# Experts' second block: half rows gathered over 128 partitions, two k tiles in each turn

## The chip, the cores and the metric

The kernel runs on one core of a Trainium2 chip. The metric is device time in microseconds (us) of one execution; a profiled execution also has a span, from its first instruction to its last. Engines are named as the profile does: PE (TensorE) with its weight loads PEld, DVE (VectorE), ACT (ScalarE), POOL (GpSimd), SP (the queue that issues most loads).

## What is computed

One transformer block over 1024 tokens of width 1024: a mixer (attention and a short convolution), then a mixture of 32 experts, four of them for each token. The change lies in the experts:

```python
def moe_ffn(h, w_router, b_router, w_gate_up, b_gate_up, w_down, b_down):
    ...
    top_logits, top_idx = lax.top_k(logits, TOP_K)
    top_w = jax.nn.softmax(top_logits, axis=-1)
    ...
    def expert_block(args):
        xe, e = args
        gu = xe @ w_gate_up[e] + b_gate_up[e]
        gate, up = jnp.split(gu, 2, axis=-1)
        gate = jnp.minimum(gate, SWIGLU_LIMIT)
        up = jnp.clip(up, -SWIGLU_LIMIT, SWIGLU_LIMIT)
        act = gate * jax.nn.sigmoid(SWIGLU_ALPHA * gate) * (up + 1)
        return act @ w_down[e] + b_down[e]
    ...
    y_rows = yb.reshape(n_rows, d) * row_w[:, None].astype(yb.dtype)
    return jnp.zeros_like(hf).at[row_tok].add(y_rows).reshape(bsz, s_len, d)
```

## The kernel before

Stages before the experts: `project_block`, `attention_block` and `mixer_block`. The mixer chooses four experts for each token and writes a list in DRAM, `list_d`, with a region of 1024 entries for each expert; an entry is (token, destination row, index of its weight). The token rows stand in `xn_d`.

`expert_block` (L1577) works through the lists in *groups*, 36 for these inputs. A group holds either one block of 128 entries (called a single turn here) or that and a second block, b = 1, of up to 64 entries (a double turn). Every matrix product is made in float32r from high and low parts, so that a weight half (512 contraction rows by 512 columns) costs block 0 twelve matmuls, `(hi, whi), (hi, wlo), (lo, whi)` for four k tiles, and block 1 eight: its high and low columns stand side by side, 64 and 64, in one stationary tile (`xt2`, `at2`). There are NH = 12 such weight halves in a group, n = 0 to 11: eight for gate and up, four for down.

The engines, each in its own loop over experts and groups:

- SP (L1731) loads the weight halves, 1 MB each, into six buffers, as DVE sets them free.
- ACT (L1887) copies a half to its high part `whi`, DVE (L2013) subtracts for the low part `wlo`, three halves ahead of PE. Both also evict PSUM.
- PE (`body`, L2199) does for each n the matmuls (L2188) and a bias product (L2170). In between it transposes: `xt(1)` (L2128) at the start of a double turn turns the gathered rows of block 1, 8 tiles of 128x128; `turn` (L2138) at n = 6 and n = 9 turns the activations, 4 tiles a block; at n = 10 `xt(0)` (L2128) turns the *next* group's 128 rows, 8 tiles.
- POOL (`body`, L1840) prepares the next group while PE works on this one. In a fixed order: `fetch` (L1767) reads the entries of both blocks from `list_d`; `stored` waits until the scatters of the group before have landed; `aim` (L1812) copies the destination rows; `gather` (L1774) waits for the entries and reads the rows from `xn_d` by an indirect DMA (L1778 is a stand-in of one column for an absent block); `weigh` (L1781) gathers the weights; L1853 copies the next destinations; `store` (L1790) waits for DVE's outputs of the group before and scatters them with an add; L1856 and L1860 end the turn.

Each POOL operation is followed by a wait of POOL for its own completion (`Chain.link`, L31). The entries' wait and the copies ahead of it read:

```python
def gather(b, g, real):
    pool.wait_ge(entry_in[b], 16 * (g + 1))
...
stored(g)
aim(own)
with pool.If(g > 0):
    for b in range(2):
        gather(b, g, b < blocks)
```

Of the kernel before, what the change touches and what calls it, by code (L numbers as in the profile page):

```python
# [6 lines left out]
ALU = mybir.AluOpType  # L7
ACT = mybir.ActivationFunctionType
# [51 lines left out]
def shared(nc, ctx, a, out):  # L60
# [27 lines left out]
    s.list_d = dram("list_d", [s.E * s.T, 3], I32)  # L88
# [15 lines left out]
def project_block(nc, s, a):  # L104
# [39 lines left out]
    with ExitStack() as ctx:  # L144
# [31 lines left out]
        nolist = qhi_all[:, 0:3 * s.E * T // P].bitcast(I32).rearrange("p (n c) -> p n c", c=3)  # L176
# [810 lines left out]
def mixer_block(nc, s, a):  # L987
# [7 lines left out]
    with ExitStack() as ctx:  # L995
# [32 lines left out]
        entry = sb("c_entry", [P, NT, K4, 3], I32)  # L1028
# [55 lines left out]
        with nc.Block() as block:  # L1084
# [45 lines left out]
            def _(pool):  # L1130
# [11 lines left out]
                for col in range(2):  # L1142
# [3 lines left out]
                                        channel_multiplier=K4))  # L1146
                pool.sem_inc(consts, 1)
# [429 lines left out]
def expert_block(nc, s, a, out):  # L1577
# [5 lines left out]
    ROWS = (P, HB)  # L1583
    GU, DN = 2 * F // SL, D // SL
# [10 lines left out]
    with ExitStack() as ctx:  # L1595
# [10 lines left out]
        xg = [sb(f"d_xg{b}", [P, D], F32) for b in range(2)]  # L1606
# [4 lines left out]
        act_t = [sb(f"d_act{b}", [P, SL], F32) for b in range(2)]  # L1611
# [6 lines left out]
        entry = [sb(f"d_entry{b}", [ROWS[b], 3], I32) for b in range(2)]  # L1618
# [4 lines left out]
        two = sb("d_two", [1, 1], I32)  # L1623
        spare = sb("d_spare", [P, 1], F32)
        colf, coli = sb("d_colf", [P, E], F32), sb("d_coli", [P, E], I32)
        turned_x = psum[:, 6:8, :].rearrange("p a (k n) -> p (a k) n", n=P)

# [51 lines left out]
        def groups_ahead(eng, body):  # L1679
# [8 lines left out]
            eng.reg_load(end, s.table[0:1, 0, 1:2])  # L1688
            eng.reg_load(two_at, s.table[0:1, 1, 0:1])
            with eng.Fori(0, E) as e:  # L1690
# [6 lines left out]
                eng.reg_mov(end, next_end)  # L1697
# [15 lines left out]
        with nc.Block() as block:  # L1713
# [44 lines left out]
            def _(pool):  # L1758
                own = Chain(pool, pool_own)
                for b in range(2):  # L1760
                    pool.dma_start(entry[b][:, :], s.list_d[b * P:b * P + ROWS[b], :]).then_inc(entry_in[b], 16)
                own.link(nc.gpsimd.memset(xg[1][HB:, :], 0.0))

                def fetch(b, e, gs, g, real):

                    at = slot_row(pool, e, gs, g, b) if real else 0
                    pool.dma_start(entry[b][:, :], s.list_d[bass.ds(at, ROWS[b]) if real else slice(0, ROWS[b]), :]  # L1767
                                   ).then_inc(entry_in[b], 16)

                def gather(b, g, real):  # L1770
                    pool.wait_ge(entry_in[b], 16 * (g + 1))
                    s.settle(pool)
                    if real:
                        pool.indirect_dma_start(out=xg[b][0:ROWS[b], :], out_offset=None, in_=s.xn_d[:, :],  # L1774
                                                in_offset=bass.IndirectOffsetOnAxis(ap=entry[b][:, 0:1], axis=0)
# [58 lines left out]
                for b in range(2):  # L1834
                    gather(b, 0, True)
# [436 lines left out]
```

## Time and profile before

| | us |
|---|---|
| median of 3 runs | 2335.89 |
| lowest, highest | 2327.54, 2337.54 |
| span of the profiled execution | 2333.4 |
| PE busy | 2204.2 (94%) |
| DVE busy | 1749.8 (75%) |
| ACT busy | 1297.3 (56%) |
| POOL busy | 867.0 (37%) |

Of the profiled execution only the span is given, no time of its own beside it; it is 2.5 us below the median. The experts' loop starts at about 711 us of the span and lasts to its end. A matmul's busy time is its whole length, with several under way at once, so intervals between starts tell more than busy sums. A timeline merges neighbouring rows of one kind: "x8" is eight of them, and its length that of all eight. The text in brackets behind a row is the idle time of its engine before it and what ended that.

### The profile page before, as it was taken

How to read it: one execution, taken by the hardware profiler on the slowest of the kernel's cores; microseconds unless marked ns; L12 is line 12 of the kernel's file. 1: busy time of each engine (PE TensorE's matmuls, PEld its weight loads, DVE VectorE, ACT ScalarE, POOL GpSimd, SP SyncE). 2: the span in 40 equal slices, each digit the busy share in tenths (PEclk: the TensorE clock that was granted, in tenths of full speed). 3: DMA queues.
4: the chain of work that ended last, by engine and by line, in shares of the span. 5: the costliest groups of instructions: out<-in, count | busy, mean ns of one | idle time of the engine just before them, and what ended most of it. 6: DMA issues, size and time to landing. Idle time of an engine off the chain costs nothing.

```text
span 2333.4 us, 36927 instructions
## 1 busy us (share of the span) xinstructions
PE 2204.2 (94%) x10506; PEld 1822.6 (78%) x10507; DVE 1749.8 (75%) x2141; ACT 1297.3 (56%) x1739; POOL 867.0 (37%) x791
## 2 busy tenths in 40 slices
PE   5999997888967999999999999999999999999997
PEld 4778885776756788888888888888888888888886
DVE  5683422776766799977689877787999778799797
ACT  4332212674225577755567755566777556576575
POOL 2262004893235243532224322242344422244251
PEclk9999997999988999999999999999999999999998
DMA  7234205873337899977689967697999868799695
GB/s 259 90 114 149 59 8 141 249 204 116 109 100 261 276 367 372 379 284 238 224 299 375 366 221 236 228 331 258 382 378 375 300 218 296 256 346 382 227 372 168
DMA packets 295170, 583.98 MB, mean 250 GB/s; under 512 B 23936, under 2 KB 45456, under 8 KB 293008
## 3 DMA queue, kind: packets, MB, share of 16 engines
q1 hardware_dynamic: 267456, 510.07, 61.3%
q0 software_dynamic: 26608, 69.07, 10.7%
q10 hardware_dynamic: 1056, 4.19, 0.5%
q8 instruction: 28, 0.46, 0.1%
q14 instruction: 22, 0.18, 0.0%
HBM read 544.79 MB, written 44.24 MB: 252 GB/s over the span
## 4 chain that ended last, share of the span: by engine, by line
PE 68%; issue 1%; DMA 0%; DVE 0%; DVEq 0%; ACT 0%; POOL 0%; ACTq 0%; POOLq 0%
PE psum L2188 62%; PE psum L2170 3%; PE psum L2128 2%; PE psum L2138 2%; DMA d_xg<-xn_d,d_entry 0%; DMA d_entry<-list_d 0%; DVE d_wlo L2013 0%; DVEq L1713 0%; POOL d_spare L1801 0%; ACT d_whi L1887 0%; DVE d_bhl L2105 0%; DVE d_raw L2112 0%; DVE d_xtlo L1992 0%; DVE d_xt L1999 0%; ACT d_xthi L1894 0%
## 5 line engine op out<-in xcount | busy, mean ns | idle before, releaser
L2013 DVE TENSOR_TENSOR d_wlo<-d_raw,d_whi 128x1024 fp32r<-128x1024 f32 x578 | 675.4, 1219 | 118.6 <-ACT d_whi L1887 117.2
L1887 ACT ACTIVATE d_whi<-d_raw 128x1024 fp32r<-128x1024 f32 x578 | 578.8, 1054 | 110.1 <-PE psum L2188 96.3
L2188 PE MATMUL psum<-d_whi,d_xthi 128*128 128x512 f32 x1152 | 454.6, 395 | 5.0 <-issue 5.0
L2188 PE MATMUL psum<-d_whi,d_xtlo 128*128 128x512 f32 x1152 | 449.5, 390 | 0.0
L2188 PE MATMUL psum<-d_wlo,d_xthi 128*128 128x512 f32 x1152 | 449.5, 390 | 0.0
L1790 POOL DMA_INDIRECT out_dram<-d_yst,d_dest x49 | 158.7, 3239 | 719.7 <-DVE d_yst L2060 666.2
L2013 DVE TENSOR_TENSOR d_wlo<-slab,d_whi 128x1024 fp32r<-128x1024 f32 x292 | 343.6, 1218 | 14.0 <-ACT d_whi L1887 12.9
L1887 ACT ACTIVATE d_whi<-slab 128x1024 fp32r<-128x1024 f32 x292 | 292.4, 1054 | 6.7 <-PE psum L2188 6.4
L2188 PEld LDWEIGHTS psum<-d_whi,d_xthi 128*128 128x128 f32 x1152 | 217.1, 188 | 50.4 <-issue 6.9
L2188 PEld LDWEIGHTS psum<-d_whi,d_xtlo 128*128 128x128 f32 x1152 | 216.8, 188 | 45.9
L2188 PEld LDWEIGHTS psum<-d_wlo,d_xthi 128*128 128x128 f32 x1152 | 217.1, 188 | 43.4
L2188 PE MATMUL psum<-d_whi,d_athi 128*128 128x512 f32 x576 | 227.7, 395 | 0.0
L2188 PE MATMUL psum<-d_whi,d_atlo 128*128 128x512 f32 x576 | 224.6, 390 | 0.0
L2188 PE MATMUL psum<-d_wlo,d_athi 128*128 128x512 f32 x576 | 224.4, 390 | 0.0
L2188 PE MATMUL psum<-d_whi,d_xt 128*128 128x512 f32 x384 | 149.7, 390 | 0.2 <-DVE d_xt L1999 0.2
L2188 PE MATMUL psum<-d_wlo,d_xt 128*128 128x512 f32 x384 | 149.7, 390 | 0.0
L1929 ACT ACTIVATE d_athi<-psum 128x512 fp32r<-128x512 f32 x72 | 43.1, 599 | 189.3 <-PE psum L2138 189.3
L1781 POOL DMA_INDIRECT d_rowt<-topw_d,d_entry x72 | 126.7, 1760 | 22.6 <-issue 21.6
L2188 PEld LDWEIGHTS psum<-d_whi,d_atlo 128*128 128x128 f32 x576 | 108.1, 188 | 23.1
L2188 PEld LDWEIGHTS psum<-d_wlo,d_athi 128*128 128x128 f32 x576 | 108.3, 188 | 21.5
L2188 PEld LDWEIGHTS psum<-d_whi,d_athi 128*128 128x128 f32 x576 | 108.4, 188 | 20.1
L2170 PE MATMUL psum<-d_bhl,d_pick 128*128 128x512 f32 (+1 forms) x288 | 115.9, 402 | 2.4 <-DVE d_pick L2066 2.4
(347 smaller groups left out, 3976.2 us busy)
## 6 DMA issues: line engine op xcount, KB each, us to landing
slab<-in_w_gate_up_dram SPq DMA_DIRECT2D x144, 1024.0 KB, 7.5
d_raw<-in_w_gate_up_dram SPq DMA_DIRECT2D x144, 1024.0 KB, 8.1
d_raw<-in_w_down_dram SPq DMA_DIRECT2D x144, 1024.0 KB, 7.2
b_wp<-in_w_ada_dram POOLq DMA_DIRECT2D x16, 1024.0 KB, 8.3
slab<-in_w_in_dram SPq DMA_DIRECT2D x12, 1024.0 KB, 5.4
a_xin<-in_x_dram ACTq DMA_DIRECT2D x2, 2048.0 KB, 14.6
slab<-in_w_ada_dram SPq DMA_DIRECT2D x4, 1024.0 KB, 13.9
v_d<-a_vst POOLq DMA_DIRECT2D x16, 256.0 KB, 2.3
```

Source lines behind the costliest of these rows:

```text
L1781: pool.indirect_dma_start(out=rowt[b][:, :], out_offset=None, in_=s.topw_d[:, :], in_offset=bass.IndirectOffsetOnAxis(ap=entry[b][:, 2:3], ...
L1790: pool.indirect_dma_start(out=s.out, out_offset=bass.IndirectOffsetOnAxis(ap=dest[b][:, :], axis=0), in_=yst[b][:, :], in_offset=None, com ...
L1887: nc.scalar.activation(whi[n % NW][:, part, :], raw[n % NRAW][:, part, :], ACT.Copy).then_inc(whi_ok, 1)
L1929: nc.scalar.activation(athi[:, 4 * i:4 * i + 4, :].rearrange("p k n -> p (k n)"), psum[:, 6, :], ACT.Copy).then_inc(athi_ok, sh)
L2013: nc.vector.tensor_tensor(wlo[n % NW][:, part, :], raw[n % NRAW][:, part, :], whi[n % NW][:, part, :].bitcast(F32), ALU.subtract).then_inc ...
L2128: mm = nc.tensor.transpose(turned_x[:, k, :], xg[b][:, k * P:(k + 1) * P], s.ident[:, :])
L2138: mm = nc.tensor.transpose(psum[:, 6 + b, t * P:(t + 1) * P], act_t[b][:, t * P:(t + 1) * P], s.ident[:, :])
L2170: mm = nc.tensor.matmul(to[0:ROWS[b], :], pick[:, 0:ROWS[b]], bhl[:, at:at + SL], start=False, stop=last)
L2188: mm = nc.tensor.matmul(to, m_[:, KH * h + k, :], w_[n % NW][:, k, :], start=(h == 0 and k == 0 and q == 0), stop=(h == 1 and k == KH - 1 ...
```

## The change

An entry gets a fourth column, twice the token's number. The second block's 64 rows of 1024 columns are gathered as 128 half rows of 512: partition r holds the first half of row r, partition 64 + r the second. For that POOL fetches the block's entries twice, into partitions 0 to 63 and 64 to 127, and adds a constant 0 or 1 to the fourth column (`half_rows`), which gives the index into `xn_halves`. The add, with its wait for block 1's entries, stands in every group, behind the fetches and ahead of `stored` and `aim`. A transposed tile of 128 columns then holds two k tiles of 64 rows, so `xt(1)` has four tiles instead of eight and `turn` two instead of four for block 1. DVE writes block 1's activations in two operations, one to each half of the partitions, and the evictions of the turned tiles read and write them in (s k) order. The memsets of the partitions that were unused fall away. The loop bound that ACT and DVE read ahead goes through a `max` with 1.

```diff
-    s.list_d = dram("list_d", [s.E * s.T, 3], I32)
+    s.list_d = dram("list_d", [s.E * s.T, 4], I32)
...
+                own.link(nc.gpsimd.iota(entry[:, :, :, 3], pattern=[[2 * P, NT], [0, K4]], base=0,
+                                        channel_multiplier=2))
...
+    HELD = ((slice(0, P),), (slice(0, HB), slice(HB, P)))
+    PARTS = (16, 32)
...
-        xg = [sb(f"d_xg{b}", [P, D], F32) for b in range(2)]
+        xg = [sb("d_xg0", [P, D], F32), sb("d_xg1", [P, D // 2], F32)]
...
-        act_t = [sb(f"d_act{b}", [P, SL], F32) for b in range(2)]
+        act_t = [sb("d_act0", [P, SL], F32), sb("d_act1", [P, SL // 2], F32)]
...
-        entry = [sb(f"d_entry{b}", [ROWS[b], 3], I32) for b in range(2)]
+        entry = [sb(f"d_entry{b}", [P, 4], I32) for b in range(2)]
...
+        xn_halves = s.xn_d.rearrange("t (h n) -> (t h) n", h=2)
...
-                eng.reg_mov(end, next_end)
+                eng.reg_alu(end, next_end, 1, ALU.max)
...
                 def fetch(b, e, gs, g, real):
 
-                    at = slot_row(pool, e, gs, g, b) if real else 0
-                    pool.dma_start(entry[b][:, :], s.list_d[bass.ds(at, ROWS[b]) if real else slice(0, ROWS[b]), :]
-                                   ).then_inc(entry_in[b], 16)
+                    if not real:
+                        pool.dma_start(entry[b][0:ROWS[b], :], s.list_d[0:ROWS[b], :]).then_inc(entry_in[b], PARTS[b])
+                        return
+                    at = slot_row(pool, e, gs, g, b)
+                    for rows in HELD[b]:
+                        pool.dma_start(entry[b][rows, :], s.list_d[bass.ds(at, ROWS[b]), :]).then_inc(entry_in[b], 16)
...
+                        src, index = (s.xn_d, entry[0][:, 0:1]) if b == 0 else (xn_halves, turned_at[:, :])
+                        pool.indirect_dma_start(out=xg[b][:, :], out_offset=None, in_=src[:, :],
+                                                in_offset=bass.IndirectOffsetOnAxis(ap=index, axis=0)
                                                 ).then_inc(xg_in[b], 16)
...
-                    own.link(nc.gpsimd.memset(act_t[1][HB:, :], 0.0))
-                    pool.sem_inc(consts, 1)
...
+                def half_rows(own, g):
+
+                    pool.wait_ge(entry_in[1], PARTS[1] * (g + 1))
+                    own.link(nc.gpsimd.tensor_tensor(turned_at[:, :], entry[1][:, 3:4], second_half[:, :], ALU.add))
+
...
                     with pool.If(g > 0):
                         for b in range(2):
                             fetch(b, e, gs, g, b < blocks)
+                        half_rows(own, g)
                     stored(g)
                     aim(own)
...
-                    nc.vector.scalar_tensor_tensor(act_t[b][0:ROWS[b], :], sg[b][:, :], CAP, up[b][:, :],
-                                                   ALU.min, ALU.mult).then_inc(act_ok, sh)
+                    if b == 0:
+                        nc.vector.scalar_tensor_tensor(act_t[0][:, :], sg[0][:, :], CAP, up[0][:, :],
+                                                       ALU.min, ALU.mult).then_inc(act_ok, sh)
+                        return
+                    for n, rows in enumerate(HELD[1]):
+                        cols = slice(n * SL // 2, (n + 1) * SL // 2)
+                        made = nc.vector.scalar_tensor_tensor(act_t[1][rows, :], sg[1][:, cols], CAP, up[1][:, cols],
+                                                              ALU.min, ALU.mult)
+                    made.then_inc(act_ok, sh)
...
-                    for k in range(KT):
+                    for k in range(KT // len(HELD[b])):
                         mm = nc.tensor.transpose(turned_x[:, k, :], xg[b][:, k * P:(k + 1) * P], s.ident[:, :])
                         if k % KH == KH - 1:
-                            mm.then_inc(xt_mm[b], 1)
+                            mm.then_inc(xt_mm[b], b + 1)
...
-                    for t in range(4):
+                    for t in range(4 // len(HELD[b])):
```

On POOL, the preparing part of a single turn before (L1767 the entry fetches, L1812 the copies, L1774 and L1778 the gathers):

```order
L1767 DMA d_entry<-list_d 128x3
L1767 DMA d_entry<-list_d 64x3
L1842 UNCONDITIONAL_BRANCH
L1806 ISA
L1812 COPY d_dest<-d_dest_next 128x1
L34 ISA
L1812 COPY d_dest<-d_dest_next 64x1
L34 REGISTER_ALU
L1847 COMPARE_AND_BRANCH
L1771 REGISTER_ALU
L1774 DMA d_xg<-xn_d,d_entry 128x1024
L1778 DMA d_xg<-xn_d 64x1
```

and in the change (`d_turned_at` is the sum that `half_rows` writes):

```order
L1788 DMA d_entry<-list_d 128x4
L1784 DMA d_entry<-list_d 64x4
L1855 REGISTER_ALU
L1856 TENSOR_TENSOR d_turned_at<-d_entry,d_second_half 128x1
L34 ISA
L1867 UNCONDITIONAL_BRANCH
L1827 ISA
L1833 COPY d_dest<-d_dest_next 128x1
L34 ISA
L1833 COPY d_dest<-d_dest_next 64x1
```

An operation that reads block 1's entries now stands between the fetches and the copies, and the gather (L1795) follows the copies as before; in a double turn's part the second fetch is there twice.

On PE, a double turn at n = 6, before, with the last matmuls of n = 5 ahead (L2138 turns `d_act`, the activations of both blocks):

```order
L2188 MATMUL psum<-d_whi,d_xt 128x512
L2188 MATMUL psum<-d_wlo,d_xt 128x512
L2134 REGISTER_ALU
L2138 MATMUL psum<-ident,d_act 128x128 x8
L2186 REGISTER_ALU
L2188 MATMUL psum<-d_whi,d_xthi 128x512
```

and in the change:

```order
L2218 MATMUL psum<-d_whi,d_xt 128x512
L2218 MATMUL psum<-d_wlo,d_xt 128x512
L2166 REGISTER_ALU
L2168 MATMUL psum<-ident,d_act 128x128 x6
L2216 REGISTER_ALU
L2218 MATMUL psum<-d_whi,d_xthi 128x512
```

Two of eight transposes are gone there and at n = 9, and `xt(1)` at the turn's start has four for eight; nothing else moves on PE.

## Rows read from the trace of the kernel before

**Rows 1.** The chain that ended last, its shares by engine.

```profile
PE 68%; issue 1%; DMA 0%; DVE 0%; DVEq 0%; ACT 0%; POOL 0%; ACTq 0%; POOLq 0%
```

**Rows 2.** Stretch: length, busy us of PE PEld DVE ACT POOL, clock, DMA share, GB/s.

```profile
1218.00:1254.00 36.00, 36.00 (x168) 29.79 (x167) 34.12 (x36) 27.02 (x31) 15.27 (x15) 1.00 1.05 385
1390.50:1451.30 60.80, 60.80 (x286) 50.28 (x285) 43.26 (x51) 32.22 (x41) 16.61 (x15) 1.00 0.70 230
```

**Rows 3.** PE timeline, line L2128: start us, us, engine, line, operation, tiles, count.

```profile
1214.14 1.04 PE L2128 MATMUL psum<-ident,d_xg 128*128 128x128 f32 x8
1250.05 1.04 PE L2128 MATMUL psum<-ident,d_xg 128*128 128x128 f32 x8
```

**Rows 4.** GpSimd timeline of one single turn, same columns, idle before and releaser.

```profile
1223.97 5.33 POOL L1790 DMA_INDIRECT out_dram<-d_yst,d_dest  x1 [11.96 <-DVE d_yst L2060]
...
1236.14 1.09 POOL L1767 DMA_DIRECT2D d_entry<-list_d  x2 [4.15 <-issue]
...
1238.10 0.97 POOL L1812 COPY d_dest<-d_dest_next 64x1 int32<-64x1 int32 x1 [0.16 <-POOL d_dest L1812]
1241.76 1.09 POOL L1774 DMA_INDIRECT d_xg<-xn_d,d_entry  x1 [2.69 <-DMA d_entry<-list_d]
```

**Rows 5.** Entry fetches: count, KB, median us to landing; then the gathers, L1774.

```profile
d_entry<-list_d POOLq DMA_DIRECT2D x36, 1.5 KB, 4.9
d_entry<-list_d POOLq DMA_DIRECT2D x36, 0.8 KB, 4.6
...
DMA to landing us min/median/max: 4.3/6.7/10.4
```

**Rows 6.** One late gather on GpSimd, its use on PE, its landing.

```profile
1664.91 2.01 POOL L1774 DMA_INDIRECT d_xg<-xn_d,d_entry  x1 [2.48 <-DMA d_entry<-list_d]
...
1673.01 1.04 PE L2128 MATMUL psum<-ident,d_xg 128*128 128x128 f32 x8
...
DMA to landing us min/median/max: 8.0/8.0/8.0
```

**Rows 7.** Waits of PE in the loop: total us, times, longest.

```profile
PEld psum L2128 <- DMA d_xg<-xn_d,d_entry: 1.2, 5, 0.3
...
PE psum L2170 <- DVE d_pick L2066: 2.4, 1, 2.4
```

**Rows 8.** An early gather with its use on PE, and all `dest` copies.

```profile
2266.10 1.03 POOL L1774 DMA_INDIRECT d_xg<-xn_d,d_entry  x1 [1.10 <-issue]
...
2275.98 1.04 PE L2128 MATMUL psum<-ident,d_xg 128*128 128x128 f32 x8
...
L1812 POOL COPY d_dest<-d_dest_next x74: 178/964/1149, 725.3 to 2301.1; 128x1 int32<-128x1 int32 x37, 64x1 int32<-64x1 int32 x37
```

**Rows 9.** PE timeline: transposes of a single and of a double turn's activations.

```profile
1237.94 0.60 PE L2138 MATMUL psum<-ident,d_act 128*128 128x128 f32 x4
...
1494.78 1.03 PE L2138 MATMUL psum<-ident,d_act 128*128 128x128 f32 x8
```

**Rows 10.** VectorE timeline at the copy of rows 4 and at rows 9.

```profile
1236.67 2.35 DVE L2013 TENSOR_TENSOR d_wlo<-d_raw,d_whi 128x1024 fp32r<-128x1024 f32 x2
...
1492.20 1.28 DVE L2032 SCALAR_TENSOR_TENSOR d_act<-d_sg,d_up 128x512 f32<-128x512 f32 x2
```

**Rows 11.** Stretches after two PE waits (columns of rows 2), and PE after the longer.

```profile
720.00:725.00 5.00, 2.62 (x12) 1.82 (x10) 4.94 (x5) 2.46 (x4) 0.55 (x1) 1.00 0.00 0
785.00:790.00 5.00, 4.99 (x14) 4.00 (x15) 2.12 (x3) 1.18 (x2) 2.81 (x4) 0.61 0.96 182
...
785.01 0.79 PE L2188 MATMUL psum<-d_whi,d_xthi 128*128 128x512 f32 x1 [5.03 <-issue]
785.61 0.63 PE L2188 MATMUL psum<-d_wlo,d_xthi 128*128 128x512 f32 x1
786.03 0.63 PE L2188 MATMUL psum<-d_whi,d_xtlo 128*128 128x512 f32 x1
```

More of the change, by code:

```diff
@@ L175, in project_block @@
         chanmean = sb("a_chanmean", [P, P], F32)
[L176 removed]
+        nolist = qhi_all[:, 0:4 * s.E * T // P].bitcast(I32).rearrange("p (n c) -> p n c", c=4)
         with ExitStack() as early:
@@ L1027, in mixer_block @@
         iota_e = sb("c_iota_e", [P, E], F32)
-        entry = sb("c_entry", [P, NT, K4, 3], I32)
+        entry = sb("c_entry", [P, NT, K4, 4], I32)
         slot = [sb(f"c_slot{i}", [P, K4], I32) for i in range(2)]
@@ L1687, in groups_ahead @@
             eng.reg_mov(start, 0)
-            eng.reg_load(end, s.table[0:1, 0, 1:2])
+            eng.reg_load(next_end, s.table[0:1, 0, 1:2])
+            eng.reg_alu(end, next_end, 1, ALU.max)
             eng.reg_load(two_at, s.table[0:1, 1, 0:1])
@@ L1696, in groups_ahead @@
                 eng.reg_mov(start, end)
-                eng.reg_mov(end, next_end)
+                eng.reg_alu(end, next_end, 1, ALU.max)
                 eng.reg_mov(two_at, next_two)
@@ L1832, in setup @@
                         pool.wait_ge(y_st[b], ST_CRED)
-                for b in range(2):
-                    gather(b, 0, True)
+                def half_rows(own, g):
+                    pool.wait_ge(entry_in[1], PARTS[1] * (g + 1))
+                    own.link(nc.gpsimd.tensor_tensor(turned_at[:, :], entry[1][:, 3:4], second_half[:, :], ALU.add))
+                gather(0, 0, True)
+                half_rows(own, 0)
+                gather(1, 0, True)
                 setup()
                 start = own.n
-                LINKS = 7
+                LINKS = 8
                 def body(e, gs, g, blocks):
-                    own = Chain(pool, pool_own, start + LINKS * g)
+                    own = Chain(pool, pool_own, start - 1 + LINKS * g)
                     with pool.If(g > 0):
@@ L1852, in body @@
                     for b in range(2):
-                        own.link(nc.gpsimd.tensor_copy(dest_next[b][:, :], entry[b][:, 1:2]))
+                        own.link(nc.gpsimd.tensor_copy(dest_next[b][:, :], entry[b][0:ROWS[b], 1:2]))
                         s.settle(pool)
@@ L1872, in _ @@
                 stored(g)
-                aim(Chain(pool, pool_own, start + LINKS * g))
+                aim(Chain(pool, pool_own, start - 1 + LINKS * g))
                 store(g)
@@ L1899, in xt_two @@
                     act.wait_ge(xt_mm[1], 2 * count)
-                    nc.scalar.activation(xt2[:, :, 0:HB], turned_x[:, :, 0:HB], ACT.Copy).then_inc(xthi_ok[1], 2)
+                    nc.scalar.activation(folded(xt2[:, :, 0:HB]), unfolded(psum[:, 6, :]), ACT.Copy).then_inc(xthi_ok[1], 2)
                 def gated(g, i, b, sh):
```

32 lines of the change are left out of this document (17 added, 15 removed).

## The prediction

> **What bounds the kernel now.** I read first the chain that ended last: TensorE is its largest part by far, 68% of the span, and no other engine reaches 1% [rows 1]. The stretch view says the same of the expert loop. A *single* turn (one block of 128 rows) fills its 36 us with PE work, and a *double* turn (128 rows and a second block of 64) fills its 60.8 us [rows 2]. The granted clock is 1.00 in both, the level of 2.4 GHz. So in steady state every TensorE instruction taken out counts, and every wait put in counts. VectorE has 34.12 of 36 us busy in single turns and 43.26 of 60.8 in double ones. The loads fill the DMA engines in single turns (share 1.05) and not in double ones (0.70).
>
> The PE timeline gives the period of a single turn: the eight transposes of the next turn's rows (`xt(0)`) start 35.91 us apart (1214.14, 1250.05) [rows 3]. There are 36 turns, 12 double and 24 single.
>
> Last I followed GpSimd around one single turn, since it fetches the rows that `xt(0)` needs [rows 4]. `xt(0)` at 1214.14; the scatter of the previous outputs starts at 1223.97, 9.83 later; the entry fetch for the next turn at 1236.14, 12.17 later; the gather at 1241.76, 5.62 later. It lands 6.7 us after its start [rows 5], at 1248.5, and `xt(0)` comes at 1250.05. The ring takes 34.3 of 35.9 us, so **a margin of about 1.6 us is all that the single turns have** although GpSimd looks two thirds idle there. It is less elsewhere: the gather at 1664.91 lasted 2.01 us and landed after 8.0, while PE took the rows at 1673.01, 8.10 after that start [rows 6]. The margin is 0.1, and the wait table already lists five short waits of weight loads for this gather, 1.2 us together [rows 7]. In double turns the same ring stands in 60.8 us, which leaves some 26.
>
> I put together all gathers that PE uses within 12 us. There are 22: 7 like the one at 1241.76 (margin 1.6), 6 like the one at 1664.91 (0.1), and 9, after a double turn or between turns of one expert, like that at 2266.10, used 9.88 later (margin 3.2) [rows 8]. The mean margin is 1.8.
>
> **The change, part by part.**
>
> *Transposes.* A double turn now has 4 instead of 8 in `xt(1)` and 6 instead of 8 in each of its two `turn` places. Eight transposes take 1.03 us and four take 0.60 [rows 9], so one costs 0.43 / 4 = 0.107 us. 8 x 0.107 = 0.86 us for a turn, 12 turns 10.3 us. In the first turn PE then waits 2.4 us for the selection matrix, which VectorE makes [rows 7]; `xt(1)` ahead of it gains nothing there (0.4). That leaves **-9.9 us**, all on the path if nothing else gives way.
>
> *Evictions and activations.* ScalarE's and VectorE's evictions have the same sizes in another order: nothing. The second block's activation on VectorE becomes two operations of half the columns. Two full ones take 1.28 us together, from 1492.20 to 1493.48, and PE turns them at 1494.78 [rows 9, 10]: 1.3 us of cover for some 0.1 us more. VectorE idles 17 us in a double turn. Nothing. If that cover went, the cost would be 24 x 0.1 = 2.4 us, which the range can hold.
>
> *The list with four columns, one more iota, the memsets, the `max` on the loop bound:* before the loop they stand beside waits of GpSimd, and they are tens of ns on other engines in the loop. Nothing, at most 1 us. In the first turn the first gather still waits for the same first entry fetch.
>
> *The new link on GpSimd.* This is the price. Before, each turn issued both entry fetches, did the two `dest` copies while they were in flight, and then waited for entry 0 and gathered. Now `half_rows` stands directly behind the fetches, in every turn, single ones too: it waits for entry **1**, adds, and only then come the wait for the stores, both copies and the gather of block 0. Behind the waiting instruction are queued the copies, both gathers, the weights' gathers and the scatter; the last two have over 10 us before the next outputs, the first gather has its margin.
>
> How late does the gather get? Count from the first fetch. The second fetch starts about 0.55 later (half of 1.09 [rows 4]) and lands 4.6 after that [rows 5], with some 0.5 for the semaphore to be seen (before, the gather starts 5.62 after the fetch, 0.7 after its entry's 4.9, and part of that is its own issue): 5.7. The add has no row. Its nearest rows are the `dest` copies on the same 128x1 columns: 0.178 at least, 0.964 median, 1.149 at most [rows 8]; I take 0.75 since an add on three columns' stride can be no cheaper than a free copy and waits like a copy. Then 0.25 of turnaround, two copies at 0.75 with 0.16 between them, and 1.10 from the last copy to the gather, the idle time of a gather that no longer waits for its entry [rows 8]. 5.7 + 0.75 + 0.25 + 0.75 + 0.16 + 0.75 + 1.1 = 9.45, against 5.62: **the gather comes 3.8 us later**. With every small operation at its shortest it is 2.0 later (5.6 + 0.2 + 0.16 + 0.18 + 0.16 + 0.18 + 1.1 = 7.6), with every one at its longest 4.8.
>
> How long such a small operation takes is set by VectorE: the copy at 1238.10 ended at 1239.07, as the pair of splits that began at 1236.67 ended at 1239.02 [rows 4, 10]. The Trainium skill (SBUF — State Buffer, "SBUF: two separate sides") says that a VectorE operation with two SBUF inputs holds the port pair shared with GpSimd for its whole length and blocks a GpSimd operation that reads SBUF. This trace agrees (0.97 us for a copy that takes 0.178 alone), and by that rule every one of the three small operations would be at its long end, which is a rival below.
>
> *What the lateness costs.* The ring goes by PE's own events, so a wait at `xt(0)` shifts all that follows, outputs and next fetch too, and comes again in the next single turn; there is nothing to catch up with. 7 x (3.8 - 1.6) + 6 x (3.8 - 0.1) + 9 x (3.8 - 3.2) = 15.4 + 22.2 + 5.4 = 43.0 us. Six of these turns are followed by a double one, whose entry 1 comes in two fetches, the third 0.55 later: 6 x 0.55 = 3.3. Longer turns spread the loads, and landings shorten from 6.7 towards the quickest, 4.3 [rows 5]; I take 0.3 of these 2.4 us, as turns lengthen by some 6%: 22 x 0.3 = -6.6. **+39.7 us.**
>
> *The clock.* After the one PE wait of 5.0 us in the loop the next 5 us were granted 0.61: the matmuls start 0.42 us apart there (785.61, 786.03 [rows 11]), while in a single turn they are (36.0 - 16 x 0.107) / 152 = 0.226 apart [rows 2]; eight slow ones cost 1.6 us. After the wait of 2.4 us the stretch stayed at 1.00, the 2.4 GHz level [rows 7, 11]. The six waits of 3.7 lie between; half the price: 6 x 0.8 = **+4.8 us**.
>
> **The sum.** -9.9 + 39.7 + 4.8 = +34.6 us, against the profiled execution's span of 2333.4: 2368.0. The median of the runs, 2335.9, is 2.5 above that span, so the forecast is **2370 us**, 1.5% slower. A measurement of this kernel can tell about 0.5% from no change.
>
> **The rivals.**
>
> *The margin swallows it; only the transposes count.* If the gather comes late by less than its margins, or lands faster by as much, no wait appears, and the time is 2335.9 - 9.9 = 2326 us. For it: at the short end the lateness is 2.0, and the six turns without margin had gathers of 2.01 us where others had 1.04, which may fall back. Against it: the median of the copies is near their long end. It decides at a lateness of 1.8 us, the mean margin; a wait of all 22 at 2.0 would be 7 x 0.4 + 6 x 1.9 = 14 us, little more than the 9.9. Chance 0.2; as 9.9 us are 0.42%, three quarters of this is "no change".
>
> *The small operations are all long, and the clock falls.* At 4.8 us: 7 x 3.2 + 6 x 4.7 + 9 x 1.6 + 3.3 = 68 us, 13 waits of over 3 us with 1.6 us of slow clock each, 21, and -9.9: +79, 2415 us. The Trainium skill (TensorE: Matmul & The Clock Gate, "What's actually happening") has the array's clock gated down by how busy PE has been; the 0.61 agrees with it [rows 11], and it makes this case dearer than its waits. Chance 0.15.
>
> *It lands somewhat earlier or overlaps more than I count.* A lateness near 2.5 gives 7 x 0.9 + 6 x 2.4 + 3.3 - 9.9 = +14, 2350 us. Chance 0.15, part of "slower" and "no change" alike.
>
> *The change doesn't do what it says:* transposes of half the tiles would still be issued. The order of instructions shows 4 and 6 for 8, so this has under 0.01.
>
> **How the numbers follow.** Forecast case (2355 to 2400) 0.5, margin 0.2, all long 0.15, in between 0.15. The likeliest gives 2370. The range takes in the margin case's time and most of the way to the long end, 2326 to 2408. Faster than 2324: 0.06 (a quarter of the margin case). Within 0.5%, up to 2347.6: the rest of that case and a third of the in-between one, 0.19. Slower: 0.75.
>
> **What would show it.** PE's rows on `d_xg` should number 344 instead of 392, and those on `d_act` 336 instead of 384; a double turn should be 0.86 us shorter. Each single turn should start GpSimd's gather 9 to 10 us after the fetch, with the add at 5.7. The wait table should have PE `d_xg` behind its DMA some 20 times, 1 to 4 us each, 35 to 50 in all, and single turns 36 to 40 us long. If that wait isn't there, the ring has a margin that I didn't see, and I am wrong by its whole size; if double turns don't shorten, transposes weren't on the path.

## The result, and the profile after

The changed kernel takes **2362.8 us** (median; 2362.0 to 2363.9), the kernel before 2334.7 in the same rounds: 1.0128 times as long, 95% interval 1.0114 to 1.0142, or 28.1 us more. The profiled execution spans 2361.2 us (before 2333.4).

First the chain that ended last, by engine, in the changed kernel:

```profile
PE 51%; issue 7%; DMA 4%; POOL 4%; POOLq 2%; DVE 1%; DVEq 0%; ACT 0%; ACTq 0%
```

Before, PE alone had 68% and GpSimd none [rows 1]. Now a path through GpSimd and its transfers has a tenth. The view of waits, PE and GpSimd over the expert loop, says where (engine, tile and line waited for, releaser, total us, times, longest):

```profile
POOL d_turned_at L1856 <- DMA d_entry<-list_d: 143.2, 35, 5.3
...
PE psum L2160 <- DMA d_xg<-xn_d,d_entry: 32.5, 13, 3.4
...
PE psum L2200 <- DVE d_pick L2098: 1.8, 1, 1.8
```

Before, only five short waits of weight loads stood there [rows 7]; now the transposes `xt(0)` themselves wait 13 times, 32.5 us in all. The half-row add (L1856) is the instruction that stands waiting for the entries, in every turn that fetches any. Three stretches, with the columns of rows 2: a single turn that ends in a wait, one that doesn't, and a double turn.

```profile
1252.90:1292.10 39.20, 36.05 (x168) 29.53 (x166) 35.81 (x37) 26.91 (x30) 16.18 (x16) 1.00 1.02 373
1216.90:1252.90 36.00, 36.00 (x167) 29.78 (x168) 32.48 (x34) 26.91 (x30) 12.91 (x16) 1.00 1.02 366
1396.70:1456.70 60.00, 60.00 (x277) 49.43 (x276) 43.72 (x53) 32.22 (x41) 14.27 (x17) 1.00 0.71 233
```

The second turn is as long as one before [rows 2], the first is 3.2 us longer at the same PE work, and the double turn is 60.0 us, 0.8 shorter. So turns with and without a wait stand side by side. GpSimd's timeline shows both. The turn with the wait (start us, us, engine, line, operation; idle before it and releaser):

```profile
1262.71 5.31 POOL L1811 DMA_INDIRECT out_dram<-d_yst,d_dest  x1 [11.98 <-DVE d_yst L2092]
...
1274.92 0.56 POOL L1788 DMA_DIRECT2D d_entry<-list_d  x1 [4.24 <-issue]
...
1280.81 1.00 POOL L1856 TENSOR_TENSOR d_turned_at<-d_entry,d_second_half 128x1 int32<-128x1 int32 x1 [4.79 <-DMA d_entry<-list_d]
1282.27 0.68 POOL L1833 COPY d_dest<-d_dest_next 128x1 int32<-128x1 int32 x1 [0.46 <-POOL d_turned_at L1856]
1283.11 0.97 POOL L1833 COPY d_dest<-d_dest_next 64x1 int32<-64x1 int32 x1 [0.16 <-POOL d_dest L1833]
1285.19 1.18 POOL L1795 DMA_INDIRECT d_xg<-xn_d,d_entry  x1 [1.11 <-issue]
```

and the turn ahead of it, without one:

```profile
1226.53 2.03 POOL L1811 DMA_INDIRECT out_dram<-d_yst,d_dest  x1 [9.93 <-DVE d_yst L2092]
...
1235.14 0.56 POOL L1788 DMA_DIRECT2D d_entry<-list_d  x1 [4.22 <-issue]
...
1243.34 1.06 POOL L1795 DMA_INDIRECT d_xg<-xn_d,d_entry  x1 [1.11 <-issue]
```

Fetch to gather is 10.27 us in the first and 8.20 in the second; before it was 5.62 [rows 4]. But the second turn's fetch also comes much earlier: `xt(0)` started at 1216.88, so it is 18.3 us behind it, against 22.1 in the first turn (`xt(0)` at 1252.85) and 22.0 before. Most of this (3.3 us) is the scatter ahead: 2.03 us instead of 5.31. PE at the end of the turn with the wait:

```profile
1288.53 0.39 PE L2218 MATMUL psum<-d_whi,d_atlo 128*128 128x512 f32 x1
1292.07 1.09 PE L2160 MATMUL psum<-ident,d_xg 128*128 128x128 f32 x8 [3.15 <-DMA d_xg<-xn_d,d_entry]
```

What the change saves is there too: the totals of PE's transposes are 344 and 336, as forecast, and four stand where eight did.

```profile
L2160 PE MATMUL psum<-ident,d_xg x344: 270/273/476, 707.4 to 2339.3; 128*128 128x128 f32 x172
...
L2168 PE MATMUL psum<-ident,d_act x336: 270/272/304, 746.8 to 2335.6; 128*128 128x128 f32 x168
```

To compare runs below I use, beside the median, the *loop*: from the start of the first `xt(0)` to that of the last that turns gathered rows, read from PE's timeline (one more behind it turns a stand-in). Before the loop, profiles differ by more than the effects sought (its start lies anywhere from 704.8 to 715.9 us), whatever the kernel. The loop was 1564.9 us before (711.06 to 2275.98) and is 1595.2 now (707.43 to 2302.62), +30.3. Its parts: +32.5 waits; +9.2 slower clock behind 5 of the waits; +1.6 in the first turn; -6.6 because the 5.03 us stall of PE at 785.01 [rows 11] and the slow stretch behind it are absent; -8.7 for the transposes in the 11 double turns behind the first (0.79 each). That makes +28.0; the other 2.3 are spread over the turns, most of them 0.05 to 0.15 us longer. What lengthens the first turn I did not find.

### The profile page after: what moved, and what is told of

It is laid out like the page before. It is cut to its first block, busy times and chain, and to the rows that moved or that the text cites. A ratio compares the mean times of both kernels' runs of the same rounds, so it can differ in the third digit from the quotient of the medians.

```text
span 2361.2 us, 36948 instructions
## 1 busy us (share of the span) xinstructions
PE 2203.7 (93%) x10410; PEld 1816.4 (77%) x10411; DVE 1760.1 (75%) x2165; ACT 1298.4 (55%) x1739; POOL 789.8 (33%) x840
## 3 DMA queue, kind: packets, MB, share of 16 engines
q0 software_dynamic: 27056, 69.26, 10.6%
## 4 chain that ended last, share of the span: by engine, by line
PE 51%; issue 7%; DMA 4%; POOL 4%; POOLq 2%; DVE 1%; DVEq 0%; ACT 0%; ACTq 0%
PE psum L2218 46%; DMA d_xg<-xn_d,d_entry 4%; PE psum L2200 2%; PE psum L2160 2%; PE psum L2168 1%; POOL d_dest L1833 1%; POOL d_roww L1886 1%; POOL out_dram L1811 1%; POOL d_spare L1822 0%; DVE d_yst L2092 0%; POOL d_entry L1788 0%; POOL d_turned_at L1856 0%; POOLq L1682 0%; POOLq L1683 0%; POOLq L1681 0%
## 5 line engine op out<-in xcount | busy, mean ns | idle before, releaser
L1811 POOL DMA_INDIRECT out_dram<-d_yst,d_dest x49 | 127.7, 2607 | 723.3 <-DVE d_yst L2092 718.6
L1955 ACT ACTIVATE d_athi<-psum 128x512 fp32r<-128x512 f32 x72 | 43.1, 599 | 189.7 <-PE psum L2168 189.7
L1802 POOL DMA_INDIRECT d_rowt<-topw_d,d_entry x72 | 96.3, 1337 | 22.6 <-issue 21.6
```

Of the source, the lines that this page charges most:

```text
L1802: pool.indirect_dma_start(out=rowt[b][:, :], out_offset=None, in_=s.topw_d[:, :], in_offset=bass.IndirectOffsetOnAxis(ap=entry[b][0:ROWS[b ...
L1811: pool.indirect_dma_start(out=s.out, out_offset=bass.IndirectOffsetOnAxis(ap=dest[b][:, :], axis=0), in_=yst[b][:, :], in_offset=None, com ...
L1955: nc.scalar.activation(athi[:, 4 * i:4 * i + 4, :].rearrange("p k n -> p (k n)"), psum[:, 6, :], ACT.Copy).then_inc(athi_ok, sh)
```

## The experiments

Two theories stood at the start. **L, the link:** block 0's gather waits behind block 1's entries, the add and the copies, and that alone costs. **H, the half rows:** more descriptors, one fetch more, wider lists and split operations cost. The stall that went with the change was a third thing to explain.

**e1_gather_first**: the changed kernel, with block 0's gather issued ahead of the add (which counts on a semaphore of its own). It computes the same.

```
                     with pool.If(g > 0):
                         for b in range(2):
                             fetch(b, e, gs, g, b < blocks)
-                        half_rows(own, g)
                     stored(g)
                     aim(own)
                     with pool.If(g > 0):
-                        for b in range(2):
-                            gather(b, g, b < blocks)
+                        gather(0, g, True)
+                        half_rows(g)
+                        gather(1, g, blocks == 2)
```

> The changed kernel with one thing moved: block 0's gather is issued ahead of POOL's wait for block 1's entries and the add of the half-row indices, which follow it. Theory L (the link is what costs: block 0's gather waits for block 1's two entry fetches, the add and the two copies): block 0's gather starts 5 to 6 us behind its fetch again instead of 10, PE's 13 waits for d_xg (32.5 us) go, and only the saved transposes are left: before less 8 to 10 us, 2322 to 2330 us. Rival H (the half rows cost: 128 descriptors in place of 64, entries fetched twice, four-column lists, activations in two operations): all of that is still there, and the time stays above 2345 us, with waits of PE in the turns that hold a second block or on DVE. Rival C (the clock lost, whatever starts the gather): above 2345 us with TensorE's granted clock below 0.975.

Measured: 2321.7 us, 0.9943 of before (0.9925 to 0.9960); loop 1553.8. PE's waits in the loop:

```profile
PE psum L2161 <- DMA d_xg<-xn_d,d_entry: 2.7, 1, 2.7
PE psum L2201 <- DVE d_pick L2099: 2.3, 1, 2.3
```

41.1 us of the changed kernel's time go with the moved lines, though every half row is still gathered; the median lies 0.3 us under the expected range. L holds, H falls as far as a kernel without the late gather is concerned. The one wait left is in a turn ahead of a double one, where three entry fetches go out and block 0's gather started 8.3 us behind the first. The five other turns of that kind gather 5.7 to 6.0 us behind it and end in no wait; why this one is late was not looked into.

**e2_wait_alone** and **e3_wait_and_add**: the other way round, the kernel before with the link alone, without and with the add (both also have the `max` on the loop bound, which e4 tests too).

```
                         for b in range(2):
                             fetch(b, e, gs, g, b < blocks)
+                        pool.wait_ge(entry_in[1], 16 * (g + 1))
+                        Chain(pool, half_own, g - 1).link(nc.gpsimd.tensor_tensor(
+                            extra[:, :], entry[1][:, 1:2], entry[1][:, 2:3], ALU.add))
```

> The kernel before with one wait added on POOL: behind the two entry fetches it waits for block 1's entries before it copies the destinations and gathers block 0. No half rows, no add, all transposes as before. (The bound of each expert's turns is also written as a maximum with 1, as the changed kernel has it.) Theory L: the gather starts 8.5 to 9.5 us behind the fetch instead of 5.6, about 0.5 to 1 us earlier than in the changed kernel, and PE waits for d_xg some 13 times by 1.5 to 3 us: 18 to 30 us of waits and 5 to 10 of slower clock, 2355 to 2370 us. Rival H: nothing of the half rows is in it, so the time is that of before, 2330 to 2342 us.

> The kernel before with the wait of the run ahead and behind it one POOL add on 64 rows of the entries, its result unused: the whole new link, without the half rows. Theory L: block 0's gather starts 10 us behind the fetch as in the changed kernel, PE waits about 13 times by 2 to 3.4 us, 30 to 34 us in all, and the transposes that the changed kernel saves (8 to 9 us) are still there: 2366 to 2376 us. Rival H: no more than before, 2330 to 2342 us. If the alternation seen in the changed kernel's trace is a property of the loop (a turn that waits lets the next turn's store and fetch start earlier), waits stand in every other turn here too.

Measured: 2365.2 us (1.0140, 1.0125 to 1.0154) and 2361.9 us (1.0135, 1.0116 to 1.0154), loops 1594.5 and 1593.8. e2 is in its range; e3 was expected 4 us higher at the least. PE's waits in e2, then in e3:

```profile
PE psum L2130 <- DMA d_xg<-xn_d,d_entry: 21.9, 11, 3.2
PE psum L2190 <- issue: 5.0, 1, 5.0
```

```profile
PE psum L2134 <- DMA d_xg<-xn_d,d_entry: 25.2, 12, 2.8
PE psum L2194 <- issue: 5.0, 1, 5.0
```

A single wait for a semaphore costs some 30 us, and **the add costs nothing that the time shows**. In the turn near 1250 us the gather starts 9.22 us behind the fetch in both. GpSimd in e2 shows why, together with e3's row:

```profile
1281.30 1.16 POOL L1813 COPY d_dest<-d_dest_next 128x1 int32<-128x1 int32 x1 [4.73 <-DMA d_entry<-list_d]
1282.63 0.97 POOL L1813 COPY d_dest<-d_dest_next 64x1 int32<-64x1 int32 x1 [0.16 <-POOL d_dest L1813]
```

```profile
1281.57 0.66 POOL L1849 TENSOR_TENSOR d_extra<-d_entry 64x1 int32<-64x1 int32 x1 [4.10 <-DMA d_entry<-list_d]
1282.68 0.68 POOL L1815 COPY d_dest<-d_dest_next 128x1 int32<-128x1 int32 x1 [0.45 <-POOL d_extra L1849]
```

The small operations end in a fixed beat here, so the added one fills time that another spent waiting (e7 below shows the beat). That is not so in every turn: in the one near 1645 us the gather comes 8.06 us behind the fetch in e2 and 9.20 in e3, a beat later. e3's waits are 3.3 us more in all, and its slow stretches of PE 3.0 us less. Here too no two single turns running end in a wait.

**e4_rest_alone**: the small parts alone on the kernel before (four-column list and iota, `max` on the bound, block 1's activation in two).

```
-                    nc.vector.scalar_tensor_tensor(act_t[b][0:ROWS[b], :], sg[b][:, :], CAP, up[b][:, :],
-                                                   ALU.min, ALU.mult).then_inc(act_ok, sh)
+                    for n in range(b + 1):
+                        cols = slice(n * SL // (b + 1), (n + 1) * SL // (b + 1))
+                        made = nc.vector.scalar_tensor_tensor(act_t[b][0:ROWS[b], cols], sg[b][:, cols], CAP,
+                                                              up[b][:, cols], ALU.min, ALU.mult)
+                    made.then_inc(act_ok, sh)
```

> The kernel before with the small parts alone: four-column list entries with their iota, the maximum on the bound of the turns, and block 1's activation as two operations of half the columns. No half rows, no wait added. I costed these at nothing: 2330 to 2340 us, and no new wait on PE. Rival H (the small parts cost): DVE's second activation, 48 of them at about 0.3 us, on the path of the 12 turns with a second block, would give up to 14 us: 2345 to 2350 us.

Measured: 2333.7 us, 1.0000 (0.9989 to 1.0012), loop 1564.8. Nothing, as costed.

**e5_transposes_twice** and **e8_after_twice**: e1 and the changed kernel with each transpose of block 1 issued twice; **e11_half_transposes**: e4 with half of block 1's transposes left out.

```
-                    for k in range(KT // len(HELD[b])):
+                    for k in (k for k in range(KT // len(HELD[b])) for again in range(b + 1)):
...
-                    for t in range(4 // len(HELD[b])):
+                    for t in (t for t in range(4 // len(HELD[b])) for again in range(b + 1)):
```

> The kernel of the run e1_gather_first with each transpose of block 1 issued twice into the same place: PE issues 8 of d_xg and 16 of d_act per turn of two blocks again, as before the change, the last of each pair with the same result. What I hold (T: the transposes are on PE's path, 0.78 us in each of 12 turns; S: the 5.0 us stall of PE near 780 us, in all profiles with the old number of transposes and in neither of those with half of them, belongs to how PE's program is laid out): T alone 2331 us, T and S 2337 us with the stall back, S without T 2328 us. If the half rows' transposes had lain beside other work: 2322 us.

> The changed kernel with each transpose of block 1 issued twice, as the run e5_transposes_twice. If the saved transposes count in the changed kernel as they do without its waits: 2372 us (T) or up to 2379 us with the stall of 5.0 us and the slower clock behind it (S). If the waits for block 0's rows take up what PE saves (the gather's time is set by POOL, not by PE), within 3 us of the changed kernel: 2360 to 2366 us, as the run e3_wait_and_add with its full transposes (2361.9 us) lets one suspect.

> The kernel of the run e4_rest_alone (before, with the small parts) with every other transpose of block 1 left out: 4 of 8 of d_xg and 2 of 4 of each d_act, so half of the second block's columns are not turned and its result is not the layer's. What the change saves on PE, without anything that it adds: by the runs e1 and e5, 0.79 us in each of 12 turns (T, 9.5 us) and the stall with the slower clock behind it (S, 6.7 us): 2317 to 2322 us, no 5.0 us stall, 27 packets. T alone: 2324 us. If these savings need something else of the half rows: 2333 us.

Measured: e5 2334.4 us (1.0004, 0.9994 to 1.0015), loop 1572.2, so 12.7 us above e1 (loop +18.3); e8 2373.0 (1.0172, 1.0147 to 1.0197), loop 1606.0, 10.2 above the changed kernel (loop +10.8); e11 2320.6 (0.9939, 0.9922 to 0.9956), loop 1548.5, 13.1 below e4 (loop -16.3). By the medians of three pairs PE's part of the change is worth 10 to 13 us, and the waits do not swallow it (my suspicion in e8's last sentence was wrong). e5 fell between its 2331 and 2337 us, e8 1 us from its T, e11 into its range. Double turns behind the first are 49.1 us from `xt(1)` to the next `xt(0)` with half the transposes and 49.9 with all, in every pair: 0.8 x 12 = 9.5 us. In the loops of the profiled executions the stall comes on top, 7.0 us for e5 against e1, which with 1.6 us of slow clock behind one wait nearly makes the 18.3. Transposes and stall together, 16.5, are more than the medians give; each median's interval is 2.5 to 6 us either way, so they don't exclude it, and only one execution of each kernel was profiled. In e5, PE in the first single turn, then e5's queue of instruction fetches (packets, MB, share):

```profile
784.65 0.79 PE L2221 MATMUL psum<-d_whi,d_xthi 128*128 128x512 f32 x1 [4.86 <-issue]
...
q8 instruction: 28, 0.46, 0.1%
```

and the same queue in e1:

```profile
q8 instruction: 27, 0.44, 0.1%
```

All kernels with the old number of transposes (before, e2, e3, e4, e5, e8) have 28 packets and the stall; the changed one, e1, e6, e7, e9, e10 and e11 have 27 and none.

**e9_sixteen_more** and **e12_sixteen_signals** ask whether it is the transposes or the length of the code.

```
                     if blocks == 2:
                         pe.wait_ge(xt_ok[0], 2 * (g + 1))
                         xt(1, g + 1)
+                        for n in range(16):
+                            pe.sem_inc(unread, 1)
                     else:
```

> The kernel of the run e1_gather_first with 16 register moves, their result unused, put behind the transposes of d_xg in PE's code for a turn of two blocks: as much code as the 8 transposes that the half rows spare there have with their weight loads (16 instructions), and none of their matrix work. Theory S (the 5.0 us stall is PE's first jump past that code into the code for a turn of one block, and with the shorter code one fetch of instructions less is made): the stall is back in the first turn of one block, the instruction queue shows 28 packets and not 27, the loop is 7 us longer: 2328 to 2332 us. If the stall hangs on the transposes themselves: 2321 to 2324 us with no stall and 27 packets; above that up to 0.8 us in each of 12 turns, should the moves stand on the path.

> The run e9_sixteen_more again with instructions that stay in the program: its register moves had no reader and were not among the executed instructions (36843, as without them). Now 16 increments of an unused semaphore stand behind the transposes of d_xg in PE's code for a turn of two blocks, as many instructions as 8 transposes with their weight loads, with no matrix work. Theory S (the length of that code decides whether one fetch of instructions more is made at PE's first jump past it): the 5.0 us stall of the first turn of one block is back, 28 packets on the instruction queue, the loop 7 us longer than in e1_gather_first and e9_sixteen_more, 2328 to 2332 us. If the transposes' matrix work or data bring the stall: 27 packets, no stall, 2321 to 2325 us, and up to 0.8 us more in each of 12 turns if the increments stand on the path.

e9's moves were optimized away: 36843 instructions ran, as in e1, so it is a repeat of e1 and nothing else (2323.5 us, 0.9953, 0.9937 to 0.9969; loop 1554.9; 1.8 us from e1). e12 measured 2349.5 us, 1.0060 (1.0040 to 1.0080), loop 1581.4. Its PE row in the first single turn, its queue, and its waits of PE:

```profile
781.10 0.79 PE L2220 MATMUL psum<-d_whi,d_xthi 128*128 128x512 f32 x1 [4.84 <-issue]
...
q8 instruction: 28, 0.46, 0.1%
...
PE psum L2220 <- issue: 16.6, 8, 4.8
```

The stall and the 28th packet are back with no matrix work added: the number of instructions decides. The first single turn is 47.7 us long in e12 and 40.4 in e1, so **stall and slow clock cost 7.3 us, once**. I had costed the increments at 0.8 us a turn at most: double turns are 50.7 to 51.1 us instead of 49.1, 1.9 for 16 of them, 0.12 each. 11 x 1.9 and 7.3 make 28, and the loop is 27.6 longer; the expected time was missed by this price. What is shown is that the stall follows the number of instructions in PE's code for a double turn. PE runs that code in the first turn and jumps over it in the next, and no run tells the two apart. The trace of before also has the 28th packet inside the stall: PE stands from 779.98 to 785.01, and the instruction queue between 784.0 and 784.2 shows

```profile
q8 instruction: 1, 0.02, 32.5%
```

that is one packet of 16 KB, about 1.0 us long (32.5% of 16 engines for 0.2 us), so it ends where the stall does, to 0.2 us. In e1 that queue has no packet between 780 and 795. What takes the 4.1 us before the packet starts stays open.

**e6_two_links**, **e7_five_links**, **e10_copies_first**: how the cost grows with the lateness. e6 and e7 are e1 with 2 or 5 useless linked copies between the entries' landing and block 0's gather; e10 is the changed kernel with the two `dest` copies ahead of the add.

```
+                def later(own, g):
+                    pool.wait_ge(entry_in[0], 16 * (g + 1))
+                    s.settle(pool)
+                    for n in range(LATER):
+                        own.link(nc.gpsimd.tensor_copy(nothing[:, :], second_half[:, :]))
+                        s.settle(pool)
...
                     aim(own)
+                    later(own, g)
                     with pool.If(g > 0):
                         gather(0, g, True)
```

```
-                        half_rows(own, g)
                     stored(g)
                     aim(own)
                     with pool.If(g > 0):
+                        half_rows(own, g)
```

> The kernel of the run e1_gather_first with two more linked copies of one column on POOL between the landing of block 0's entries and its gather, in every turn; nothing else. Each copy takes 0.2 to 1.3 us with its turnaround, so the gather starts some 2 us later. Theory L with the margins now read (landing 1.4 us ahead of PE's need in turns behind a turn of one block, near 3 behind one of two): waits of PE of about 0.6 us in every second of those turns, 2324 to 2330 us. Were every microsecond of the link paid from the first, in 22 turns, it would be 2365 us.

> As the run ahead with five copies: the gather starts some 4 to 6 us later than in the run e1_gather_first, as much as in the changed kernel, without its wait for block 1's entries and its add. Theory L: the same waits as in the changed kernel, in every second single turn, and 2352 to 2372 us. Rival N (no alternation: every turn that leads to a gather pays the lateness less its margin, 22 times 3.3 us): above 2390 us. Rival W (it is the wait for block 1's entries that costs, not the lateness): 2322 to 2330 us.

> The changed kernel with POOL's two copies of the destinations ahead of the wait for block 1's entries and the add, both gathers behind them: the copies lie beside the fetches' landing again, only the wait and the add stay in the link. The gather starts 6.5 to 7.5 us behind the fetch (5.7 before, 10.2 changed, 8.0 with two links added). Theory L, from the run with two links (12 us for 2.3 us of lateness, loop 10.6): 2323 to 2332 us, the likeliest 2327. If each turn's wait for block 1's entries costs by itself: 2345 us and more.

PE's waits in the loop, in e10, e6 and e7:

```profile
PE psum L2160 <- DMA d_xg<-xn_d,d_entry: 5.4, 5, 2.8
```

```profile
PE psum L2172 <- DMA d_xg<-xn_d,d_entry: 10.0, 8, 2.8
```

```profile
PE psum L2172 <- DMA d_xg<-xn_d,d_entry: 33.7, 13, 4.6
```

Fetch to gather is read in the single turn near 1250 us, in e6 the one ahead of it (in e2 and e3 the transposes and the stall of before are in the time, so their loop stands against e4's 1564.8, the others' against e1's 1553.8):

| run | fetch to gather | waits, us | loop, more | median |
|---|---|---|---|---|
| e1 | 5.8 | 1, 2.7 | 0 | 2321.7 |
| e10 | 6.8 | 5, 5.4 | 5.1 | 2327.9 |
| e6 | 8.0 | 8, 10.0 | 10.6 | 2334.1 |
| e2 | 9.2 | 11, 21.9 | 29.7 | 2365.2 |
| e3 | 9.2 | 12, 25.2 | 29.0 | 2361.9 |
| changed | 10.3 | 13, 32.5 | 41.4 | 2362.8 |
| e7 | 10.7 | 13, 33.7 | 50.6 | 2370.4 |

e10 came within 1 us of its likeliest value (0.9965, 0.9951 to 0.9979). e6's median came out 4 us above its range (1.0002, 0.9990 to 1.0014), e7's (1.0148, 1.0126 to 1.0169) inside, far from both rivals: without block 1's entries in its way the late gather costs the same, and not 22 times. Beyond a fetch to gather of some 8 us the price climbs faster than the waits, in part as slow stretches come behind them. e7's copies show the beat that e3 suggested, GpSimd's rows and then VectorE's:

```profile
1280.57 0.68 POOL L1838 COPY d_nothing<-d_second_half 128x1 int32<-128x1 int32 x1 [1.89 <-DMA d_entry<-list_d]
1281.41 0.97 POOL L1838 COPY d_nothing<-d_second_half 128x1 int32<-128x1 int32 x1 [0.16 <-POOL d_nothing L1838]
1282.55 0.97 POOL L1838 COPY d_nothing<-d_second_half 128x1 int32<-128x1 int32 x1 [0.16 <-POOL d_nothing L1838]
1283.68 0.97 POOL L1838 COPY d_nothing<-d_second_half 128x1 int32<-128x1 int32 x1 [0.16 <-POOL d_nothing L1838]
1284.82 0.18 POOL L1838 COPY d_nothing<-d_second_half 128x1 int32<-128x1 int32 x1 [0.16 <-POOL d_nothing L1838]
```

```profile
1279.98 4.63 DVE L2051 TENSOR_TENSOR d_wlo<-d_raw,d_whi 128x1024 fp32r<-128x1024 f32 x4 [0.67 <-ACT d_whi L1925]
1284.53 0.68 DVE L2064 TENSOR_SCALAR d_up<-psum 128x512 f32<-128x512 f32 x1
```

Four splits take 4.63 us, one every 1.14. Four copies end at 1281.25, 1282.38, 1283.52 and 1284.65, one for each split; the fifth, beside an operation that reads PSUM, takes 0.18. The Trainium skill (SBUF — State Buffer, "SBUF: two separate sides") has the port pair locked for the whole of such a VectorE instruction, and the trace agrees to 0.1 us: each of the four copies ends as a split does.

The version that beats both kernels is e1: 11.9 us below before and 41.1 below the changed one.

## Why the prediction came out

**The transposes: right, and more came with them.** I took 9.9 us; the double turns give 0.8 each, 9.5 in all. What I did not see is that shorter code would also take away the stall of [rows 11], which I used only as a sample of the slow clock. That is 7.3 us by e12 and e1 (6.6 in the changed kernel's own turn). PE's part was -15 in the loop (-8.7 and -6.6), not -10; the medians of the pairs say 10 to 13.

**Evictions, activations, list, bound: right at nothing.** e4 shows 0.0 us. VectorE's two operations are 0.414 us each, 0.83 where one was 0.68, inside its cover.

**The link: the mechanism right, its lateness too small.** The step "the gather comes 3.8 us later (9.45)" measured 10.27 - 5.62 = 4.6 us. Its terms: the add starts 5.89 behind the fetch (5.7 taken), takes 1.00 (0.75), then 0.46 of turnaround (0.25), copies of 0.68 and 0.97 (0.75 each), 0.16, and 1.11 to the gather (1.1). That is nearly the "all long" rival's 4.8 (added up with the longest copy, 1.149 us, three times, that rival is 5.0 us late).

**"It comes again in the next single turn; there is nothing to catch up with": wrong.** This is the step that failed. By my own margins a lateness of 4.6 gives 7 x 3.0 + 6 x 4.5 + 9 x 1.4 = 61 us. The trace shows 32.5 in 13 waits instead of 22. In the two turns shown above, the one that follows a wait has its fetch 3.8 us earlier, gathers 26.5 us behind its `xt(0)` instead of 32.3, and ends in no wait. None of the 9 single turns that follow a wait ends in one (periods 35.95 to 36.01 us, but for two in which the clock was lower). Eight of the nine have a short scatter (1.7 to 2.0 us); the ninth, at 884.74, has the long one but fetches early anyway (19.9 us behind its `xt(0)`, as before). So in this kernel a late turn is followed by an early one. It is no law: in e8 one single turn behind a wait of 3.29 us ends in another, of 0.39. The two errors, a lateness put too low and turns put too many, nearly cancelled, 39.7 forecast against 32.5, and that is luck.

**The clock: too small, and for the wrong reason.** I took 4.8 us, half a price for each of six waits. It was 9.2: about 1.7 (once 2.7) behind each of five waits and nothing behind the other eight. Stretches after a wait of 2.00 us and after one of 2.05 (columns of rows 2):

```profile
1548.50:1553.50 5.00, 5.00 (x20) 4.08 (x19) 3.65 (x4) 4.03 (x5) 0.00 (x0) 0.66 1.05 404
...
1683.90:1688.90 5.00, 5.00 (x26) 4.28 (x27) 3.58 (x5) 4.35 (x6) 0.00 (x0) 1.00 1.05 407
```

The waits are equal, but 1.00 is the 2.4 GHz level throughout and 0.66 has part of its 5 us at 1.2 GHz. The length of the wait doesn't decide alone; what does stays open.

**The sum.** Forecast -9.9 + 39.7 + 4.8 = 34.6; the loop gives -8.7 - 6.6 + 32.5 + 9.2 + 1.6 + 2.3 = 30.3, and the medians 28.1. Sign and size came out (2370 said, 2362.8 measured) with the dominant term near by two errors that cancel, and three others off in both directions. The margin rival fell in the changed kernel. Near its own lateness the cost is small, as it says: with 1.0 us (e10) only 5.1 us of loop appear, with 2.2 (e6) 10.6, where I had put 14 at 2.0. e6 is level with the kernel before (2334.1 us), so the turning point lies near 2.2 us, and I had put it at 1.8. The forecast signs held otherwise: 60.0 us double turns, gather 10 behind the fetch, the add at 5.9, single turns of 36 to 39.4 us, and of 40.1 to 43.1 behind a double turn; of "20 waits, 35 to 50 us" there were 13 with 32.5.

## What to carry to other kernels

Before adding a wait to a queue, follow the oldest work behind it: here one wait for an entry that block 0 does not need cost 30 us in e2, and issuing block 0's gather first turned a loss of 28 us into a gain of 12. Measure such a ring's margin in turns, not as an average, and check whether a late turn changes the phase of the next one before multiplying by the number of turns. And when instructions leave a loop, look at stalls marked "issue" and at the packets of the instruction queue, since 16 instructions moved one here.

## What the hardware showed that I had not expected

- **The number of instructions on PE.** 16 more or less in the code for a double turn decide whether the first single turn stalls 4.8 to 5.0 us and runs 7.3 us longer (28 or 27 packets on the instruction queue).
- **An added GpSimd operation can be free or cost a whole beat, and a late entry is dear.** Small operations end with VectorE's splits, 1.14 us apart, so gathers start in steps: 30.1, 31.2, 32.3 us behind `xt(0)` in e2, e3, the changed kernel and others.
- **The scatter takes 2.03 or 5.31 us** for the same rows. In the changed kernel it is 5.3 where it starts 0.83 to 0.84 us after VectorE's run of splits begins and 2.0 where it starts 0.71 to 0.75 after, and it is 2.0 only behind a wait of PE. The short scatter makes the next fetch early, and with it the waits alternate. But neither the phase nor the wait decides alone. The rows are the changed kernel's behind the wait that ends at 884.74, which starts 0.83 after, and one of e5, which starts 0.85 after and behind no wait. What sets the length is not shown.

```profile
894.39 5.33 POOL L1811 DMA_INDIRECT out_dram<-d_yst,d_dest  x1 [13.24 <-DVE d_yst L2092]
```

```profile
2121.94 1.90 POOL L1812 DMA_INDIRECT out_dram<-d_yst,d_dest  x1 [10.50 <-DVE d_yst L2093]
```

- **A bare semaphore increment on PE costs 0.12 us** in a full stream (16 in 1.9 us, e12).
- **The clock fell to 0.66 to 0.69 behind some 2 us waits and not behind others.** Behind a wait of 3.23 us (959.98) it was 0.50, behind another of 3.23 (1759.13) 1.00. e2 and e3 with waits of the same sort lost 4.6 and 1.6 us by it, e7 16.
